# Norms of a two-layer diffusion trunk: residual update and squares ahead of the next weight split, the last down piece signalled bank by bank

## The reference

```python
h  = rmsnorm(x, g_norm1) * (1 + scale1) + shift1        # norms 0 (layer 0) and 2 (layer 1)
...                                                     # four mixers from h @ w_in, merged by gates
x  = x + gate1 * (merged @ w_o)
h2 = rmsnorm(x, g_norm2) * (1 + scale2) + shift2        # norms 1 (layer 0) and 3 (layer 1)
f  = swiglu(h2, w_ff_gate, w_ff_up, w_ff_down)          # layer 0: dense, hidden width 3584
f  = top-2-of-8 expert swiglu(h2)                       # layer 1
x  = x + gate2 * f
```

## Time and profile before

| | |
|---|---|
| median of three runs | 1802.79 us (1801.98 to 1804.7) |
| the profiled execution | 1802.86 us, of it 1801.0 us span |
| TensorE busy | 1712.3 us, 95% of the span |
| VectorE busy | 650.1 us, 36% |
| ScalarE busy | 521.3 us, 29% |
| GpSimd busy | 92.1 us, 5% |
| granted TensorE clock, mean | 0.978 of full |
| read from memory | 521.93 MB, 291 GB/s over the span |

### The profile page before, as it was taken

One profiled execution on the slowest core, in us unless ns is written; L12 is line 12 of the kernel. 1 busy time (PEld: TensorE's weight loads), 2 busy tenths in 40 slices (PEclk: granted clock), 3 DMA queues, 4 the chain that ended last, 5 costly groups with the idle time before them and its releaser, 6 DMA issues.

```text
span 1801.0 us, 31768 instructions
## 1 busy us (share of the span) xinstructions
PE 1712.3 (95%) x14239; PEld 1049.0 (58%) x14239; DVE 650.1 (36%) x1037; ACT 521.3 (29%) x828; POOL 92.1 (5%) x105
## 2 busy tenths in 40 slices
PE   5999998999999899999899999999999899988998
PEld 2899986999999789998433333333333333323333
DVE  3487675444344667776400020212112011020112
ACT  3445533433333445543200111112111111211211
POOL 4020041000000010031000000000000000000000
PEclk8999998999999899999899999999999999999999
DMA  9364586677765544446777899999999999999992
GB/s 350 125 240 147 192 300 217 221 267 264 280 229 201 189 144 150 141 156 215 288 281 291 318 389 400 399 399 395 399 400 400 400 398 397 396 398 398 397 396 109
DMA packets 208632, 525.71 MB, mean 292 GB/s; under 512 B 5205, under 2 KB 11555, under 8 KB 201329
## 3 DMA queue, kind: packets, MB, share of 16 engines
q1 hardware_dynamic: 206240, 519.68, 77.4%
q0 software_dynamic: 2256, 4.01, 0.9%
HBM read 521.93 MB, written 1.74 MB: 291 GB/s over the span
## 4 chain that ended last, share of the span: by engine, by line
PE 82%; DMA 8%; DVE 6%; ACT 2%; POOL 1%; issue 1%; SPq 0%; ACTq 0%; DVEq 0%; POOLq 0%
PE ps L2003 13%; PE ps L1562 10%; PE ps L2049 10%; PE ps L1563 10%; PE ps L1564 10%; PE ps L2009 6%; PE ps L1990 5%; DMA e_raw<-in_w_e_gate_dram 4%; PE ps L1997 3%; PE ps L1568 3%; PE ps L2044 2%; PE ps L1956 2%; DVE wlo L972 2%; PE ps L1626 1%; PE ps L2065 1%; DMA raw<-in_w_e_gate_dram 1%
## 5 line engine op out<-in xcount | busy, mean ns | idle before, releaser
L1562 PE MATMUL ps<-acts_hi,whi 128*128 128x256 f32 x1600 | 463.6, 290 | 18.4 <-DVE wlo L972 5.6
L1563 PE MATMUL ps<-acts_lo,whi 128*128 128x256 f32 x1600 | 455.1, 284 | 0.0
L1564 PE MATMUL ps<-acts_hi,wlo 128*128 128x256 f32 x1600 | 454.9, 284 | 0.0
L972 DVE TENSOR_TENSOR wlo<-raw,whi 128x1024 fp32r<-128x1024 f32 (+1 forms) x220 | 265.0, 1247 | 189.7 <-ACT whi L647 189.6
L1562 PEld LDWEIGHTS ps<-acts_hi,whi 128*128 128x128 f32 x1600 | 309.0, 193 | 38.0 <-issue 24.6
L1563 PEld LDWEIGHTS ps<-acts_lo,whi 128*128 128x128 f32 x1600 | 309.2, 193 | 0.8 <-issue 0.7
L1564 PEld LDWEIGHTS ps<-acts_hi,wlo 128*128 128x128 f32 x1600 | 309.2, 193 | 0.0
L647 ACT ACTIVATE whi<-raw 128x1024 fp32r<-128x1024 f32 (+1 forms) x220 | 219.9, 1050 | 84.3 <-PE ps L1564 35.8
L1997 PE MATMUL ps<-e_raw,KTt 128*32 128x512 f32 x504 | 219.8, 592 | 1.8 <-DMA e_raw<-in_w_e_gate_dram 1.8
L2003 PE MATMUL ps<-e_raw,KTt 128*32 128x512 f32 x1464 | 214.3, 592 | 0.0
L1529 DVE TENSOR_TENSOR big<-ps,big 96x512 f32<-96x512 f32 x28 | 19.2, 686 | 380.3 <-ACT big L902 380.3
(11 more groups left out here) (309 smaller groups left out, 2048.7 us busy)
## 6 DMA issues: line engine op xcount, KB each, us to landing
e_raw<-in_w_e_up_dram SPq DMA_DIRECT2D x39, 2048.0 KB, 19.4
e_raw<-in_w_e_gate_dram SPq DMA_DIRECT2D x38, 2048.0 KB, 23.9
e_raw<-in_w_e_down_dram SPq DMA_DIRECT2D x37, 2048.0 KB, 19.4
raw<-in_w_ada_dram SPq DMA_DIRECT2D x24, 2048.0 KB, 8.2
raw<-in_w_in_dram SPq DMA_DIRECT2D x22, 2048.0 KB, 9.0
raw<-in_w_e_down_dram SPq DMA_DIRECT2D x19, 2048.0 KB, 19.2
raw<-in_w_e_gate_dram SPq DMA_DIRECT2D x18, 2048.0 KB, 23.6
raw<-in_w_e_up_dram SPq DMA_DIRECT2D x17, 2048.0 KB, 19.4
```

What stands on the lines that cost most here:

```text
L972: tt(w, part, h.bitcast(F32), ALU.subtract).then_inc(lo_piece, 1)
L1562: mm(out, a_hi, b_hi, start=start, stop=False, skip_group_check=shared)
L1563: mm(out, a_hi, b_lo, start=False, stop=False, skip_group_check=shared)
L1564: return mm(out, a_lo, b_hi, start=False, stop=stop, skip_group_check=shared)
```

## The change

For halves with norm 1 or 2 ahead of them, `task(H - 1)` comes before the split of half H on both engines. ScalarE then does the first piece's rounding, the root, the second piece's rounding, and then the roundings of the norm. VectorE does the mean, the first piece's remainder, and then the norm, in which the second piece's remainder stands in the first turn of the loop over pairs, behind that pair's activation remainder. Apart from this, the last down piece signals a new semaphore `ff_sum` after j = 1, 3 and 5, and VectorE waits for these ahead of the updates of banks 4, 5 and 6, and for the whole piece ahead of bank 7's alone. No instruction with data is added or removed.

```diff
--- before.py
+++ after.py
@@ -393,11 +393,11 @@
              "probs_turned probs_kept o_done o_scaled o_turned o_hi o_lo b_ready b_hi b_lo cf_used "
              "conv_v conv_ready ln_sum ln_sq_done ln_sqsum ln_ms ln_sdone ln_z ln_th ln_o d_hi d_lo "
              "stored").split())
-        (ff_act_done, ff_hid_done, ff_hi, ff_lo, ff_read, lg_done, h2_turned, h2_kept,
+        (ff_sum, ff_act_done, ff_hid_done, ff_hi, ff_lo, ff_read, lg_done, h2_turned, h2_kept,
          mask_done, pos_done, tab_done, staged, sel_done, selT_t, selT_kept, xe_t, xe_kept,
          gate_done, up_done, part_done, up_parted, up_sum, e_hid, e_turn, e_kept, down_done, y_parted, y_first, y_kept, sc_fill,
          res_turned, res_kept, sc_gated, pair_exp, item_added, out_ready, y_stored) = map(sem, (
-             "ff_act_done ff_hid_done ff_hi ff_lo ff_read lg_done h2_turned h2_kept "
+             "ff_sum ff_act_done ff_hid_done ff_hi ff_lo ff_read lg_done h2_turned h2_kept "
              "mask_done pos_done tab_done staged sel_done selT_t selT_kept xe_t xe_kept "
              "gate_done up_done part_done up_parted up_sum e_hid e_turn e_kept down_done y_parted y_first y_kept sc_fill "
              "res_turned res_kept sc_gated pair_exp item_added out_ready y_stored").split())
@@ -857,17 +857,21 @@
             norm_root(0)
             keep_ada(3)
             for H in range(HALVES):
+                n = norm_before(H)
                 if H > 1:
                     for a in units_before(H - 1):
                         keep_ada(a)
-                for c_ in range(2):
-                    hi(H, c_)
-                if H:
+                if n:
                     task(H - 1)
-                n = norm_before(H)
+                    hi(H, 0)
+                    norm_root(n)
+                    hi(H, 1)
+                else:
+                    for c_ in range(2):
+                        hi(H, c_)
+                    if H:
+                        task(H - 1)
                 if n is not None:
-                    if n:
-                        norm_root(n)
                     norm_hi(n)
                     if n == 2:
                         act.wait_ge(stored, 64)
@@ -1026,7 +1030,7 @@
                 dve.wait_ge(sd_done, n + 1)
                 link(dve.reciprocal(rstd, rstd))
 
-            def norm_apply(n):
+            def norm_apply(n, H=None):
 
                 norm_scale(n)
                 norm_root_inverse(n)
@@ -1037,6 +1041,8 @@
                         ins = norm_unit(k + 2)
                         if n < 3:
                             norm_lo(n, k)
+                            if k == 0:
+                                lo(H, 1)
                         link(ins)
                         norm_modulate(n, k + 2)
                     elif n < 3:
@@ -1353,8 +1359,11 @@
 
                 if hh == FFN_HALVES - 1:
 
-                    dve.wait_ge(piece_used, ff_used("down", CHUNKS - 1))
                     for j in range(KT):
+                        if j == KT - 2:
+                            dve.wait_ge(piece_used, ff_used("down", CHUNKS - 1))
+                        elif j % 2 == 0:
+                            dve.wait_ge(ff_sum, j // 2 + 1)
                         for g in range(2):
                             r = xT[:, j, TOK * g:TOK * g + TOK]
                             a = 256 * (j % 2) + TOK * g
@@ -1374,16 +1383,18 @@
             norm_mean(0)
             first_norm()
             for H in range(HALVES):
-                if H:
+                n = norm_before(H)
+                if H and not n:
                     for c_ in range(2):
                         lo(H, c_)
                     task(H - 1)
                 for a in units_before(H - 1) if H > 1 else ():
                     keep_modulation(a)
-                n = norm_before(H)
                 if n:
+                    task(H - 1)
                     norm_mean(n)
-                    norm_apply(n)
+                    lo(H, 0)
+                    norm_apply(n, H)
             task(HALVES - 1)
             norm_mean(3)
             norm_apply(3)
@@ -1866,6 +1877,8 @@
                             ins = mm3(ps[:, 4 + j // 2, NT * (j % 2):NT * (j % 2) + NT],
                                       wh[:, 0, P * j:P * j + P], wl[:, 0, P * j:P * j + P],
                                       br_hi[:, x, :], br_lo[:, x, :], first and j % 2 == 0, last, shared=True)
+                            if last and j in (1, 3, 5):
+                                ins.then_inc(ff_sum, 1)
                     else:
                         bank = 2 * (kind == "up") + q
                         for k in range(KT):
```

## The result

The changed kernel took 1798.51 us, median of 8 runs (1796.74 to 1801.25), against 1804.13 of the kernel before in the same comparison: ratio 0.9971, 95% interval 0.9962 to 0.9979. In a second comparison on another occasion it was 1798.37 and 0.9966 (0.9953 to 0.9978). The medians of the two comparisons lie 5.6 and 5.2 us apart; the first interval goes from 3.8 to 6.9 us.

The account below looks back on a forecast made before the run. TensorE was taken as the bound (82% of the chain), losing time only standing still or at half clock. Gains of 2.66 at norm 1 and 2.30 at norm 2, 4.96 us, from 1802.86 gave 1797.9, range 1795.0 to 1801.0.

Parts of the forecast that it names:

- Norm 1's order: Norm 1: update ahead of the split brings the mean 4.63 us earlier; remainders cost 0.79 and 1.18; fourth pair 2.66 earlier.
- The pieces behind it: Behind norm 1's fourth pair: TensorE works without a gap, so 2.66 us carries through; full clock at restart would add up to 2.0.
- The rest of the kernel: Feed-forward, mixer and experts: moved and not changed, the same durations about 5 us earlier.
- The sign that I had named for being wrong as a whole: Experts not starting earlier by the gain, or their stage's loads ending at the same time.
- Norm 2's signals: Norm 2: with signals by bank, VectorE's sixteen updates start at 580.17, 2.47 us earlier than 582.64.
- rival (b): Norm 2: signals or updates held until the piece ends, moved remainders make it 1.3 us slower; 1801.5 us, chance 0.06.
- Norm 2's sum and remainders: Norm 2: mean 3.90 us earlier, less 0.62 before the reciprocal and 0.98 in the loop: next half 2.30 earlier.
- The rule weighed: ScalarE's roots: drain of about 1.38 us per table switch would take 1.3 and 0.8 off the gain; rows spoke against it.
- (c): Rival, ScalarE in both norms: drain makes load to root 1.38 us longer and the reciprocal waits; 1800.0 us, chance 0.03.
- (a): Rival, both norms' sums: the clock's fall was an accident, most executions had it full; gain 2.6, 1800.3 us, chance 0.14.
- (d): Rival, first pieces after the norms: shorter holes keep the clock up; 1794.9 us, chance 0.08.
- (e): Rival, restarts and mixer behind: stretched pair distance drops TensorE to 1.2 GHz, about 3 us per thirty products; 1806.9, chance 0.05.

Follow-up runs that it names:

- e4_norm2_only: Kernel before with the new order and the signals by bank at norm 2 alone, norm 1 as before: 1799.48 us, ratio 0.9984.
- e3_norm1_only: Kernel before with the new order at norm 1 alone, norm 2 as before, without signals: 1801.65 us, ratio 0.9986.
- e1_no_bank: Changed kernel without the signals by bank, VectorE waiting for the whole last down piece, new order kept at both norms: 1800.90 us, ratio 0.9985 to before.
- v2: Changed kernel with norm 2's roundings ahead of the squares and both its remainders ahead of the mean: 1795.63 us, ratio 0.9950 to before.
- v3_both_free: Changed kernel with both norms' weight remainders moved out of the chain into VectorE's idle time: 1794.92 us, ratio 0.9949 to before.
- v3_again: Repeat of the changed kernel with all four weight remainders in VectorE's idle time: 1794.85 us, ratio 0.9952 to before.
- e2_bank_only: Kernel before with the signals and waits by bank alone, order of the splits unchanged: 1803.81 us, ratio 1.0001.
- f1_filler: Kernel before with small unread fp32 products in TensorE's waits for the squares at both norms: 1803.98 us, ratio 0.9999.
- v4_busy: Changed kernel with all four remainders in idle time, plus small unread products in TensorE's holes around both norms: 1794.36 us, ratio 0.9949 to before.

## Why the prediction was right

**Norm 1's order.** Right in size. Predicted 2.66 at the fourth pair, measured 2.89 (2.05 against e4_norm2_only, whose old norm 1 had full clock in the sum). The term for the clock, 1.0, measured 0.94 to 0.95, and it is a gain only in executions in which the clock would have fallen. The costs were right too: mean to reciprocal 1.68 (1.77 said), first distance of pairs 3.46 (3.5 said). The root was ready at 296.76 (296.34 + 0.42), ahead of the remainder's end, so it was covered as said.

**The pieces behind it.** The step that was open. I carried the fourth pair's gain through to the end; the Silu gained 2.38, and 3.2 in e3_norm1_only. The half pace at the restart (clock 0.50 in 314 to 316) lasts longer or shorter, by 1.3 us between kernels with equal pairs (6.41 in both traces of the changed kernel, 5.66, 5.60 and 5.13 in e1, e3 and v2), and by 0.46 between the two traces of one kernel (6.26 in v3_both_free, 5.80 in v3_again).

**The rest of the kernel.** I took it as moved and not changed, and that was off by 1.5 us: the clock fell in the mixer of layer 1, and from norm 2's mark to the first expert load it took 202.5 instead of 201.05. It is not the new order at norm 2 by itself that does it: e3_norm1_only has 202.54 with the old one, e4_norm2_only 201.93, e2_bank_only 201.07. What sets off the fall stays open. The sign that I had named for being wrong as a whole did not appear: the expert loads started 4.34 and ended 4.56 earlier.

**Norm 2's signals.** Right to a hundredth: updates 2.48 earlier (2.47 said). VectorE needs 4.23 for the sixteen while TensorE writes the other banks, 4.22 before with TensorE idle, so reading beside writing costs nothing here. e1_no_bank and e2_bank_only show that rival (b)'s price was right and its mechanism was not at work.

**Norm 2's sum and remainders.** Mean 3.82 earlier (3.90 said), reciprocal lost 0.50 (0.62 said), the loop 0.91 (0.98 said): 2.41 against 2.30.

**What I had not counted, and where luck came in.** In the old order the updates at norm 2 wait for the weights of the next half, and their landing moves from one kernel's execution to another's: the updates started 0.64, 0.86, 1.01 and 1.88 after the last product in the four traces with the old norm 2 (before, e2, e3, f1). The profiled execution of before was the luckiest of them. In the changed kernel the landing is out of the chain, -1.84 or -1.83 in every trace. It did not cost the old order much, though: where the updates were later the sum of squares was shorter (in f1_filler by its filling), and the next half came at 23.50, 23.65, 23.69 and 23.54. So it adds 0.2 at most to the gain.

The whole lies closer to the forecast than its parts allow me to claim. In the two traces the norms gained 4.8 and the mixer gave 1.5 back, 3.3 in all, and the 1.03 ahead of norm 1 is an accident; the medians differ by 5.6 and 5.2, and the interval (3.8 to 6.9) holds 4.96 but not 3.3. The profiled execution of before, from which I subtracted, took 1802.86, and the median of the eight runs is 1804.13. What those other executions had lost more is not shown, since the kernel before was traced only once; the clock in norm 1's sum, which differs between executions by 0.94, and in the mixer, which differs between traces by 1.5, are of that size. That 4.96 was met to a microsecond is in part luck.

**The rule weighed, and the rivals.** In norm 2 the table load starts at 582.45, 0.02 behind the end of the rounding (581.55 + 0.88), and the root at 583.74, 0.01 behind the end of the load, so (c) is out. The Trainium skill (ScalarE: Activation LUTs, What ACT_TABLE_LOAD costs) puts about 1.38 us of drain beside the load at every switch; this trace does not agree, it has 0.03 us on both sides of the load together. (a) was half right: in norm 1's sum the fall is there in two traces of three and worth 0.94; in norm 2 the old order loses 1.2 by it each time. (d) needs products in the holes, v4_busy; in the changed kernel's two traces it did not come by itself. (e) came in part. The clock behind norm 1 fell at 303, behind the first pair, where before it fell at 312.4, with the third. From the fourth pair to the Silu it took 0.51 more, and the mixer behind lost 1.5, together 2.0 us where (e) had 3 for each group of thirty products and three such groups.

## What to carry to other kernels

Where an in-order engine has both the end of one stage and the preparation of the next to do, put the end first only if its data are ready first; here neither the order nor the finer signal brought anything at norm 2 without the other: the order alone lost 1.1 us there, the signal alone changed nothing. Then look for the idle time into which the preparation fits: the same splits, put into gaps ahead of the mean and behind norm 1's last pair instead of into the chain, were worth another 3.5 us. When a change is a few microseconds in 1800, measure its step from the last product ahead of it: in the changed kernel those distances repeat to 0.02 us, while the whole moves by 4 to 5. In the old order, where a load stands in the chain and the clock falls in some executions, they moved by 0.8 at norm 1's mean and 1.2 at norm 2's updates, so look at more than one trace, and look behind the changed place too.

## What the runs showed of the hardware that I had not expected

- The same 1664 KB load, issued by SyncE with nothing else of the queue under way, landed after 6.6 to 7.0 us in twelve traces and after 7.8 in one, and this sets a chain's start when the load is only just in time.
- With ten to 22 small instructions of fp32 ones by ones between two bursts, 0.12 to 0.13 us each, TensorE's clock stayed at 2.4 GHz in the one trace of v4_busy; from the fourth pair to the Silu it then took 4.30 us instead of 5.1 to 6.4.
- TensorE's clock can fall behind one and the same wait in one kernel and not in another: behind the 3.37 us wait in the mixer of layer 1 it fell in both traces of the changed kernel (0.50 and 0.66 in 658 to 662) and not in that of before (1.00), and cost 1.5 us.
- VectorE reads one PSUM bank while TensorE accumulates into the next, without either slowing: 0.26 us per update and 0.12 us per product as without the other.
